# Second block's feed-forward on one core: the first gate and up tile from inputs without norm factor and shift

## The reference, cut to what matters

```
def modulate(h, shift, scale):
    return h * (1 + scale) + shift
...
x = x + g1 * mix                                   # mix ends in "@ w_out"
h2 = modulate(rmsnorm_2(x, norm2_g[layer]), sh2, sc2)
x = x + g2 * swiglu(h2, w_ffn_gate[layer], w_ffn_up[layer], w_ffn_down[layer])
```

## Time and profile before

| | |
|---|---|
| median of 3 runs | 2545.27 us (2544.14 to 2551.4) |
| the profiled execution: its own time | 2544.38 us |
| span of its profile | 2542.6 us |
| PE busy | 2499.6 us, 98% of the span |
| POOL busy | 1787.5 us, 70% |
| DVE busy | 1134.4 us, 45% |
| ACT busy | 585.2 us, 23% |

### The profile page before, as it was taken

One profiled execution on the slowest core, in us unless ns is written; L12 is line 12 of the kernel. 1 busy time (PEld: TensorE's weight loads), 2 busy tenths in 40 slices (PEclk: granted clock), 3 DMA queues, 4 the chain that ended last, 5 costly groups with the idle time before them and its releaser, 6 DMA issues.

```text
span 2542.6 us, 33829 instructions
## 1 busy us (share of the span) xinstructions
PE 2499.6 (98%) x11958; PEld 2028.0 (80%) x11958; DVE 1134.4 (45%) x1660; ACT 585.2 (23%) x1006; POOL 1787.5 (70%) x816
## 2 busy tenths in 40 slices
PE   8999999999999999999999999989999999899999
PEld 6877788788888787778878888868888788688887
DVE  7764423644454756442364445746138722311100
ACT  3233312311110323331231111132224520211100
POOL 6766777688888576677768888736353467588887
PEclk9999999999999999999999999999999999999999
DMA  4222223233355222222323335411122222233233
GB/s 142 91 83 82 83 91 99 67 99 99 109 203 185 75 91 83 80 86 91 98 101 99 97 109 199 166 51 59 50 67 84 74 79 97 69 97 99 94 117 104
DMA packets 70208, 250.84 MB, mean 99 GB/s; under 512 B 8304, under 2 KB 8432, under 8 KB 70000
## 3 DMA queue, kind: packets, MB, share of 16 engines
q1 hardware_dynamic: 66528, 239.69, 28.9%
q10 hardware_dynamic: 3600, 9.99, 1.1%
HBM read 247.56 MB, written 2.10 MB: 98 GB/s over the span
## 4 chain that ended last, share of the span: by engine, by line
PE 90%; issue 4%; DVE 3%; POOL 2%; DMA 1%; ACT 0%; SPq 0%; POOLq 0%; DVEq 0%; ACTq 0%
PE bank L488 23%; PE bank L484 22%; PE bank L485 22%; PE bank L430 4%; PE bank L432 4%; PE bank L431 4%; PE bank L796 1%; POOL w_hi L399 1%; PE bank L1149 1%; PE bank L821 1%; PE bank L805 1%; POOL w_lo L402 1%; PE bank L1133 1%; DMA w_raw<-weights 1%; PE bank L1123 1%
## 5 line engine op out<-in xcount | busy, mean ns | idle before, releaser
L399 POOL TENSOR_TENSOR w_hi<-w_raw,one 128x1024 fp32r<-128x1024 f32 x405 | 780.8, 1928 | 714.5 <-PE bank L488 438.7
L402 POOL TENSOR_TENSOR w_lo<-w_raw,w_hi 128x1024 fp32r<-128x1024 f32 x405 | 1008.3, 2490 | 31.8
L484 PE MATMUL bank<-act_hi,w_hi 128*128 128x512 f32 x1808 | 714.8, 395 | 2.9 <-POOL w_hi L399 2.7
L485 PE MATMUL bank<-act_lo,w_hi 128*128 128x512 f32 x1808 | 705.8, 390 | 0.0
L488 PE MATMUL bank<-act_hi,w_lo 128*128 128x512 f32 x1872 | 464.3, 389 | 0.0
L488 PEld LDWEIGHTS bank<-act_hi,w_lo 128*128 128x128 f32 x1872 | 350.8, 188 | 73.6 <-issue 1.0
L484 PEld LDWEIGHTS bank<-act_hi,w_hi 128*128 128x128 f32 x1808 | 340.5, 188 | 81.2 <-issue 9.4
L485 PEld LDWEIGHTS bank<-act_lo,w_hi 128*128 128x128 f32 x1808 | 340.7, 188 | 73.6 <-issue 3.8
L484 PE MATMUL bank<-f_hi,w_hi 128*128 128x512 f32 x528 | 207.2, 392 | 1.4 <-POOL w_hi L399 1.3
L485 PE MATMUL bank<-f_lo,w_hi 128*128 128x512 f32 x528 | 205.6, 389 | 0.0
L488 PE MATMUL bank<-f_hi,w_lo 128*128 128x512 f32 x528 | 131.8, 390 | 0.0
(11 more groups left out here) (447 smaller groups left out, 3524.9 us busy)
## 6 DMA issues: line engine op xcount, KB each, us to landing
w_raw<-weights SPq DMA_DIRECT2D x405, 512.0 KB, 3.4
mod_raw<-mods SPq DMA_DIRECT2D x48, 512.0 KB, 4.5
bias<-bias ACTq DMA_DIRECT2D x8, 512.0 KB, 4.1
resid<-x SPq DMA_DIRECT2D x8, 256.0 KB, 5.3
out<-resid ACTq DMA_DIRECT2D x8, 256.0 KB, 4.4
params<-params ACTq DMA_DIRECT2D x2, 534.5 KB, 4.1
ctx_raw<-ctx ACTq DMA_DIRECT2D x1, 1024.0 KB, 4.9
second<-second ACTq DMA_DIRECT2D x1, 972.5 KB, 6.9
```

The source lines that it names most:

```text
L399: nc.gpsimd.tensor_tensor(w_hi[:, j, :], w_raw[:, j, :], one[:, 0:1].to_broadcast([P, 1024]), ALU.mult)\
L402: nc.gpsimd.tensor_tensor(w_lo[:, j, :], w_raw[:, j, :], w_hi[:, j, :].bitcast(F32), ALU.subtract).then_inc(blocks_split, 1)
L484: mm(out, w_hi[:, slot, tile * P:tile * P + P], rows_hi, start=start, stop=False)
L485: mm(out, w_hi[:, slot, tile * P:tile * P + P], rows_lo, start=False, stop=False)
```

## The change

G1 and U1 are multiplied from inputs that hold gain2 alone. ACT makes raw_hi = resid * gain2 beside the squares, DVE raw_lo, during w_out, and PE multiplies G1 and U1 with these. Since the factor r belongs to a token (a column of the bank) and the shift to a feature, W(raw * r + shift) = (W raw) * r + W shift: the bank is multiplied by r when DVE reads it, and W shift comes from 16 extra matmuls of 2 columns for each of the two blocks (shift_parts holds the shift's high and low part) in bank 4, as a bias for each output feature. Seven of the eight sums of squares move between the blocks of w_out. G2 is the first block that reads act_hi and act_lo. The root's table is loaded ahead of w_out's squares.

```diff
+            def first_from_raw(b0, odd):
+                for j in range(2):
+                    b, slot = b0 + j, (j + odd) % 2
+                    pe.wait_ge(hi_split, b + 1)
+                    for k in range(KT - 1):
+                        pe.wait_ge(raw_lo_ready, 8 * DEPTH + k + 1)
+                        high_parts(bank[j][:, :], slot, k, raw_hi[:, k, :], raw_lo[:, k, :], k == 0)
+                    take(b)
+                    for k in range(KT - 1):
+                        low_part(bank[j][:, :], slot, k, raw_hi[:, k, :], False)
+                    pe.wait_ge(shift_ready, 2)
+                    for w in (w_hi, w_lo):
+                        for k in range(KT):
+                            mm(bank[4][:, 2 * j:2 * j + 2], w[:, slot, k * P:k * P + P], shift_parts[:, k, :],
+                               start=(w is w_hi and k == 0), stop=(w is w_lo and k == KT - 1))
+                    if j == 0:
+                        x_norm_sum(2 * DEPTH + 1, KT - 1)
+                    pe.wait_ge(raw_lo_ready, 8 * DEPTH + KT)
+                    product(bank[j][:, :], slot, KT - 1, raw_hi[:, KT - 1, :], raw_lo[:, KT - 1, :], False, True)\
+                        .then_inc(blocks_done, 1)
...
+                if from_raw:
+                    first_from_raw(b0, odd)
+                    free(2, ordinal(2))
+                    pe.wait_ge(hi_split, b0 + 3)
+                    for k in range(KT):
+                        pe.wait_ge(lo_ready, lo0 + k + 1)
+                        high_parts(bank[2][:, :], odd, k, act_hi[:, k, :], act_lo[:, k, :], k == 0)
+                    take(b0 + 2)
+                    for k in range(KT):
+                        last = low_part(bank[2][:, :], odd, k, act_hi[:, k, :], k == KT - 1)
+                    last.then_inc(blocks_done, 1)
+                    pairs(0, (3,))
...
-            w_out(DEPTH, B2_OUT, use_2, merge_2, B2_OUT % 2)
-            x_norm_sums(2 * DEPTH + 1)
+            w_out(DEPTH, B2_OUT, use_2, merge_2, B2_OUT % 2,
+                  then=lambda m: x_norm_sum(2 * DEPTH + 1, m - 1) if m > 0 else None)
...
-            x_squares(2 * DEPTH + 1, lambda k: act.wait_ge(bank_free[k % 4], use_2("out", k % 4, k // 4, 0) + 2))
+            run(root[:, 5:6], ones[:, 0:1], ACT.Sqrt)
+            for k in range(KT):
+                act.wait_ge(bank_free[k % 4], use_2("out", k % 4, k // 4, 0) + 2)
+                act.wait_ge(x_summed, 8 * (2 * DEPTH + 1) + k + 1)
+                run(squares[k % 2], resid[:, k, :], ACT.Square).then_inc(x_sq, 1)
+                run(raw_hi[:, k, :], resid[:, k, :], ACT.Copy, scale=gain2[:, k:k + 1]).then_inc(raw_hi_ready, 1)
             x_norm(2 * DEPTH + 1)
             apply_hi_mod(1, M_SHIFT2)
+            act.wait_ge(ffn_bias_ready, 1)
+            act.wait_ge(bank_free[0], use_2("ffn", 0, 0, 0) + 2)
+            run(tmp[:, 0, :], tmp[:, 0, :], ACT.Silu, bias=ffn_bias[:, 0:1]).then_inc(silu_done, 1)
+            act.wait_ge(f_ready, FT * DEPTH + 1)
+            run(f_hi[:, 0, :], tmp[:, 2, :], ACT.Copy).then_inc(f_hi_ready, 1)
...
+            def raw_low_2(k):
+                dve.wait_ge(raw_hi_ready, 8 * DEPTH + k + 1)
+                v.scalar_tensor_tensor(raw_lo[:, k, :], resid[:, k, :], gain2[:, k:k + 1],
+                                       raw_hi[:, k, :].bitcast(F32), ALU.mult, ALU.subtract).then_inc(raw_lo_ready, 1)
 
-            add_gated(B2_OUT, 1, M_GATE1, "out")
+            add_gated(B2_OUT, 1, M_GATE1, "out", raw_low_2)
             x_norm(2 * DEPTH + 1)
             apply_mod(2 * DEPTH + 1, gain2, M_SHIFT2)
+
+            dve.wait_ge(lo_ready, 8 * (2 * DEPTH + 2))
+            dve.wait_ge(blocks_done, B2_FFN + 1)
+            v.tensor_tensor(tmp[:, 0, :], bank[0][:, :], rstd_row, ALU.mult).then_inc(bank_free[0], 1)
+            dve.wait_ge(blocks_done, B2_FFN + 2)
+            did(v.tensor_copy(bias_parts[:, :], bank[4][:, 0:4]))
+            v.tensor_tensor(ffn_bias[:, :], bias_parts[:, 0:4:2], bias_parts[:, 1:4:2], ALU.add).then_inc(ffn_bias_ready, 1)
+            v.tensor_tensor(tmp[:, 2, :], bank[1][:, :], rstd_row, ALU.mult).then_inc(bank_free[1], 1)
+            dve.wait_ge(bank_free[1], use_2("ffn", 1, 0, 0) + 2)
+            dve.wait_ge(ffn_bias_ready, 1)
+            dve.wait_ge(silu_done, FT * DEPTH + 1)
+            v.scalar_tensor_tensor(tmp[:, 2, :], tmp[:, 2, :], ffn_bias[:, 1:2], tmp[:, 0, :], ALU.add, ALU.mult)\
+                .then_inc(f_ready, 1)
+            dve.wait_ge(f_hi_ready, FT * DEPTH + 1)
+            v.tensor_tensor(f_lo[:, 0, :], tmp[:, 2, :], f_hi[:, 0, :].bitcast(F32), ALU.subtract).then_inc(f_lo_ready, 1)
             ffn(B2_FFN, lambda b: use_2("ffn", b, 0, 0), FT * DEPTH)
```

More of the change, by code:

```diff
@@ L165, in build @@
         totals, decay = keep("totals", [P, 4, 8]), keep("decay", [P, 4, 8])
+        shift_parts = keep("shift_parts", [P, KT, 2], F32R)
+        bias_parts, ffn_bias = keep("bias_parts", [P, 4]), keep("ffn_bias", [P, 2])
         phase = (top[0] - 128 + 511) // 512 * 512 + 128
@@ L324, in build @@
         ctx_loaded, second_loaded, part_done = sem("ctx_loaded"), sem("second_loaded"), sem("part_done")
+        shift_ready, ffn_bias_ready = sem("shift_ready"), sem("ffn_bias_ready")
         swap_loaded, mods_first, mod_copied, ctx_rstd = (
@@ L553, in first_two @@
                         last.then_inc(blocks_done, 1)
+            def first_from_raw(b0, odd):
[18 more added lines that the diff above has]
+                        .then_inc(blocks_done, 1)
             def ffn(b0, lo0, ordinal, down_ordinal, f0, odd=0, norm=None, post_norm=None, ahead=None,
-                    within=None):
+                    within=None, from_raw=False):
                 def pairs(i, js):
@@ L563, in ffn @@
                     free(j, ordinal(j))
-                first_two(b0, [bank[0][:, :], bank[1][:, :]], lo0, odd, norm=norm)
-                pairs(0, (2, 3))
+                if from_raw:
[10 more added lines that the diff above has]
+                    pairs(0, (3,))
+                else:
+                    first_two(b0, [bank[0][:, :], bank[1][:, :]], lo0, odd, norm=norm)
+                    pairs(0, (2, 3))
                 with pe.Fori(1, FT // 2) as i:
@@ L596, in merging, with w_out @@
                             last.then_inc(at_done if j == 0 else blocks_done, 1)
-            def w_out(l, b_out, which, at, odd=0, norm=None):
+            def w_out(l, b_out, which, at, odd=0, norm=None, then=None):
                 _, _, _, _, m_hi, m_lo, _ = at
@@ L611, in w_out @@
                                       norm=norm if m == KT - 1 else None)
+                    if then is not None:
+                        then(m)
             def take_bank(name):
@@ L1232, in _ @@
             merging(DEPTH, B2_BRA, use_2, merge_2, B2_BRA % 2)
-            w_out(DEPTH, B2_OUT, use_2, merge_2, B2_OUT % 2)
-            x_norm_sums(2 * DEPTH + 1)
+            w_out(DEPTH, B2_OUT, use_2, merge_2, B2_OUT % 2,
+                  then=lambda m: x_norm_sum(2 * DEPTH + 1, m - 1) if m > 0 else None)
             ffn(B2_FFN, 16 * DEPTH + 8, lambda b: use_2("ffn", b, 0, 0), lambda b: use_2("down", b, 0, 0), FT * DEPTH,
-                B2_FFN % 2)
+                B2_FFN % 2, from_raw=True)
         @block.scalar
@@ L1294, in ffn, with one @@
             def ffn(b0, ordinal, f0):
-                with act.Fori(0, FT // 2) as i:
+                def one(i, j):
+                    act.wait_ge(blocks_done, b0 + 4 * i + 2 * j + 1)
+                    run(tmp[:, j, :], bank[2 * j][:, :], ACT.Silu).then_inc(bank_free[2 * j], 1)
+                    act.wait_ge(bank_free[2 * j + 1], ordinal(2 * j + 1) + i + 2)
+                    run(f_hi[:, 2 * i + j, :], tmp[:, 2 + j, :], ACT.Copy).then_inc(f_hi_ready, 1)
+                one(0, 1)
+                with act.Fori(1, FT // 2) as i:
                     for j in range(2):
[L1297 to L1300, removed]
+                        one(i, j)
             def ffn_scaled(b0, ordinal, f0):
@@ L1773, in ffn, with one @@
             def ffn(b0, ordinal, f0):
-                with dve.Fori(0, FT // 2) as i:
-                    for j in range(2):
[L1776 to L1783, removed]
+                def one(i, j):
+                    dve.wait_ge(blocks_done, b0 + 4 * i + 2 * j + 2)
+                    dve.wait_ge(bank_free[2 * j], ordinal(2 * j) + i + 2)
+                    dve.wait_ge(f_lo_ready, f0 + 2 * i + j + 1)
+                    v.tensor_tensor(tmp[:, 2 + j, :], tmp[:, j, :], bank[2 * j + 1][:, :], ALU.mult)\
+                        .then_inc(bank_free[2 * j + 1], 1)
+                    dve.wait_ge(f_hi_ready, f0 + 2 * i + j + 1)
+                    v.tensor_tensor(f_lo[:, 2 * i + j, :], tmp[:, 2 + j, :], f_hi[:, 2 * i + j, :].bitcast(F32),
+                                    ALU.subtract).then_inc(f_lo_ready, 1)
+                one(0, 1)
+                with dve.Fori(1, FT // 2) as i:
+                    for j in range(2):
```

(14 more changed lines are left out.)

## The result

| | before | changed |
|---|---|---|
| median of 9 runs each, side by side | 2544.43 us (2540.03 to 2551.67) | 2551.93 us (2548.78 to 2554.69) |
| the profiled execution | 2544.38 us | 2554.69 us |
| its span | 2542.6 us | 2552.8 us |

The ratio is 1.0026, with a 95% interval of 1.0015 to 1.0037: 4 to 9 us slower, which at the bound of 0.3% is no change. In a second session the same kernel, word for word, gave 2548.60 against 2547.85 us, ratio 1.0000 (0.9986 to 1.0014).

What follows compares the result with a forecast made beforehand. PE, busy for 98% of the span, was taken as the bound. G2 ending 1.9 us later through lost turns plus 1.3 us of clock made 3.2 us slower, forecast 2548 us, range 2542 to 2552.5.

Steps and rivals of the forecast that it cites:

- Sums in w_out: Sums of squares moved between w_out's blocks cost 0.87 us each; they only change place, nothing is saved.
- G1 and U1: Both blocks run at full clock without a pause; 16 small matmuls add 1.70 us to each, at 0.106 us apiece.
- rival C: Small shift matmuls cost their upper bound, 1.5 us more ahead of the last sum; 5 us slower, 2550; chance 0.08.
- The chain to act_lo: From the last sum, 6.8 us to the first pair and 8.7 us for the pairs; with turns, last act_lo at 2196.1.
- The turns: In apply_mod, DVE instructions with two SBUF inputs and POOL's splits exclude each other: 0.8 us at first tmp, 4.3 at U2's split.
- Rival B: DVE keeps its turn against POOL in apply_mod, only 0.8 us lost; 0 to 3 us faster, 2542.5 to 2545; chance 0.30.
- The clock: PE, nearly idle during G2's wait, falls to half clock; slow products cost 0 to 3.4 us, taken as 1.3.
- The rest: Seven instructions reading out banks 0, 1 and 4, the final feed-forward work and the early root table cost nothing.
- The signs: Expected in the after profile: no 6.69 us pause before G1, 8 to 11 us idle before G2's products, long DVE instructions, half clock.

Runs made afterwards that it cites:

- sums_moved_only: The kernel before with seven of eight sums of squares between w_out's blocks, nothing else; stretch (w_out's block 1 w_lo products to U2's first product) 69.04 against 69.0 us.
- hold_u2_split: The changed kernel, but POOL begins the split of U2's weights only when the last act_lo is made; stretch 68.05 us against 71.2, median 2541.82 us.
- psum_apply: The changed kernel with apply_mod's reciprocal and tmp tiles in PSUM, so no DVE instruction of it reads two SBUF tensors; stretch 68.01 us, ratio 0.9994.
- changed_again: The changed kernel once more, word for word, against the kernel before in a second session; stretch 71.72 us, median 2548.60 against 2547.85 us, ratio 1.0000.

## Why the prediction was right, point by point

The forecast was 2548, no measurable change, with 1.9 us of lost turns and 1.3 us of clock in the stretch; measured were 2.2 and 2.7 us in the stretch, and 2551.93 and 2548.60 us as medians.

- *Sums in w_out.* Predicted 0.87 us each and nothing won. In the changed kernel a block with its sum takes 6.34 us (2168.98 to 2175.32), 5.44 before, so 0.90. sums_moved_only shows that nothing is won.
- *G1 and U1.* The small matmuls come every 0.10 us (2180.98 to 2181.79 for eight), where I took 0.106 from the earlier trace rows; rival C is out. G1 took 8.1 us from the end of the sum before it to U1's first product, predicted 8.0; U1 7.3, predicted 7.15.
- *The chain to act_lo.* Predicted: last act_lo 28.1 us behind G1's start. Measured: 27.5 (2176.2 to 2203.7).
- *The turns.* Predicted 0.8 us at the first tmp and 4.3 at U2's split. Measured: the first pair of tmp 2.19 us instead of 1.41, so 0.8; and 2.38 + 2.83 less 2 x 0.74, so 3.7. The 4.3 were too much by 0.6: the prediction took the whole of both POOL instructions as lost and a full 0.66 us for each DVE instruction behind them, and these end 0.53 and 0.55 us after POOL's. That is 0.2 of the 0.6; what makes the rest isn't shown. hold_u2_split and psum_apply each removed this from a different side. Rival B, that DVE keeps its turn, is out: w_hi began at 2191.86, while an act_lo ran, and ended at 2194.19, before the tmp that had started at 2192.34.
- *The clock.* It fell as predicted, to 0.50 in 2197.53 to 2204.74. The term was too large in this profile: the ten products behind the last act_lo took 2.8 us (2203.85 to 2206.66) instead of 2.27, so 0.5 us instead of 1.3, since full clock had returned when the eight w_lo products ran. In changed_again, with the same turns, they took 3.34 us, so 1.1, and that is the 0.5 us by which its stretch is longer.
- *The rest* was hidden, as said: bank 0 was read out at 2203.69, before U2 began. (The instructions that read out the banks are six, not seven.)
- *The signs.* All came but one: PE's idle time ahead of G2's w_lo products is 5.0 us in all (0.25, 4.32 and 0.41 in the last three stretches shown), not 8 to 11. At half clock the products count as busy for nearly all the time between two act_lo (6.80 of 7.21 us in the last stretch).

What the prediction didn't see is how much of a median is decided by half clock elsewhere. Its range held, but by 0.6 us in the first comparison, and before's own 35 runs beside changed_again go from 2539.66 to 2555.35 us. The sum for the stretch, 3.2 against 2.2 and 2.7 us, is borne out by its parts; that the median of 2551.93 fell inside the range is partly luck, for most of its distance to before's isn't in the sum.

## What to carry to other kernels

A stall on one engine often keeps a second engine quiet, and a third one lives from that quiet: before filling a pause, look which engines are idle in it, and what they will do to each other once the pause is filled. Where GpSimd works in the background all the time, put one of two tensor operands of VectorE into PSUM wherever they sit on the path; it cost some 0.8 us here, for two tmp tiles instead of four, and together with an earlier start of the chain it made the difference between 71.2 and 62.6 us. And when an effect is a few microseconds in 2500, measure the stretch in the trace as well as the median, and don't read the one as the other.

## What the runs showed of the hardware that I had not expected

- A DVE instruction in its turn behind POOL can last 2.9 us for 0.75 us of work. POOL pays too where it stands between two such instructions: w_lo 2.67 us instead of 2.39, w_hi 2.33 instead of 1.89 (beside a raw_lo of 2.9 us w_lo stayed at 2.40).
- Where the inputs lie decides, not the instruction: the same scalar_tensor_tensor with 512 elements took at most 0.756 us with one PSUM input while POOL worked, and the reciprocal, with one SBUF input, took 3.35 us beside POOL's w_hi and w_lo (2184.64 to 2187.99 in the changed kernel), as it did in before with POOL idle.
- The same kernel ran a stretch of 55 us at a mean granted clock of 0.88 in one execution and 1.00 in another; PE was busy in all of it both times (55.00 of 55 us).
